# A hybrid decoder step: q and k turned and split in the projection instead of in attention

## The reference, cut to what matters

```
h = rmsnorm(x);  q, k, v, g, z, xbc, dt = split(h @ w_in)        # 1024 x 7696
q, k = rmsnorm per head(q), rmsnorm per head(k)                  # k is also an output
for (window, d) in (128, 1), (512, 4), (2048, 16):               # dilated attention
    query i reads keys i, i-d, i-2d, ..., i-window;  scores * 1/8 + T5 bias(distance)
merge the three outputs by their softmax denominators
a = attention * silu(g)
s = gated rmsnorm(SSD scan(silu(conv(xbc)), dt), z)
y = x + [a, s] @ w_out
```

## Time and profile before

| | us |
|---|---|
| runs (3) | 3159.28, 3165.08, 3168.09; median 3165.08 |
| the profiled execution, its own time | 3156.04 |
| its span, first to last instruction | 3154.4 |
| TensorE matmul busy | 2724.5 (86%) |
| DVE busy | 1305.9 (41%) |
| ACT busy | 941.5 (30%) |
| POOL busy | 788.3 (25%) |
| mean granted TensorE clock | 0.933 of full |

### The profile page before, as it was taken

How to read it: one execution, slowest core, us unless ns; L and a number is a source line. 1 busy time by engine, 2 the same in 40 slices (tenths; PEclk the granted TensorE clock), 3 DMA queues, 4 the chain that set the end, 5 groups by cost and what they waited for, 6 DMA issues and landing times. The chain is left out here.

```text
span 3154.4 us, 48044 instructions
## 1 busy us (share of the span) xinstructions
PE 2724.5 (86%) x16822; PEld 2410.5 (76%) x16822; DVE 1305.9 (41%) x3359; ACT 941.5 (30%) x1999; POOL 788.3 (25%) x533
## 2 busy tenths in 40 slices
PE   7999999999999999978988989889709999505699
PEld 7899999999988888668888878888607888402585
DVE  3254444000000354355656656656326666374321
ACT  3211111221111112125555555545415454200100
POOL 1065565121221231000222122221314434242000
PEclk9999999999999999989999989989959999757899
DMA  4221212321211111182746556464245655383532
GB/s 154 85 75 57 72 58 91 114 70 58 69 58 63 67 53 54 42 148 42 135 73 119 97 86 127 75 107 78 56 146 180 208 199 191 109 310 146 203 146 80
DMA packets 450512, 339.24 MB, mean 108 GB/s; under 512 B 351924, under 2 KB 400412, under 8 KB 442381
## 3 DMA queue, kind: packets, MB, share of 16 engines
q1 hardware_dynamic: 432268, 275.90, 32.6%
q0 software_dynamic: 15424, 56.69, 5.6%
q10 hardware_dynamic: 2672, 4.74, 0.4%
HBM read 242.87 MB, written 99.79 MB: 109 GB/s over the span
## 5 line engine op out<-in xcount | busy, mean ns | idle before, releaser
L118 PE MATMUL bank<-w_hi,hT_hi 128*128 128x256 f32 x1792 | 506.0, 282 | 13.6 <-ACT stage L524 4.7
L120 PE MATMUL bank<-w_hi,hT_lo 128*128 128x256 f32 x1792 | 504.8, 282 | 0.9 <-issue 0.8
L119 PE MATMUL bank<-w_lo,hT_hi 128*128 128x256 f32 x1792 | 503.1, 281 | 0.0
L1059 PE MATMUL obank<-turned_p,v_in 128*128 128x128 f32 (+1 forms) x1632 | 342.1, 344 | 103.2 <-DVE turned_p L1139 97.0
L1059 PEld LDWEIGHTS obank<-turned_p,v_in 128*128 128x128 f32 x1632 | 265.2, 204 | 126.6 <-DVE turned_p L1139 65.2
L118 PEld LDWEIGHTS bank<-w_hi,hT_hi 128*128 128x128 f32 x1792 | 338.8, 189 | 17.3 <-issue 5.6
L120 PEld LDWEIGHTS bank<-w_hi,hT_lo 128*128 128x128 f32 x1792 | 339.4, 189 | 0.0
L119 PEld LDWEIGHTS bank<-w_lo,hT_hi 128*128 128x128 f32 x1792 | 338.7, 189 | 0.0
L1029 PE MATMUL front<-k_hi,q_st 128*128 128x256 f32 x768 | 303.9, 406 | 4.5 <-DVE k_lo L1099 2.8
L1117 DVE CUSTOM_DVE_ANT_0 score<-front,bias_sb 128x256 f32<-128x256 f32 (+1 forms) x768 | 244.5, 362 | 137.6 <-issue 135.6
L602 DVE TENSOR_SCALAR xc<-xc_in,cw,cb 128x2048 f32<-128x2048 f32 x12 | 16.2, 1347 | 642.8 <-ACT xc_in L553 642.8
(11 more groups left out here) (273 smaller groups left out, 5123.7 us busy)
## 6 DMA issues: line engine op xcount, KB each, us to landing
w_raw<-w_in POOLq DMA_DIRECT2D x26, 1024.0 KB
q_in<-q SPq DMA_DIRECT2D x32, 512.0 KB
k_in<-k_out SPq DMA_DIRECT2D x32, 512.0 KB
v_in<-v_out SPq DMA_DIRECT2D x32, 512.0 KB, 7.4
cum_all<-cum SPq DMA_DIRECT2D x16, 1024.0 KB, 7.6
xcT<-xc SPq DMA_DIRECT2D x12, 1024.0 KB, 3.9
xc_chunk<-xcT SPq DMA_DIRECT2D x8, 1536.0 KB, 12.0
kt_d<-cache_k SPq DMA_DIRECT2D x24, 512.0 KB, 8.4
```

The costliest lines, as they stand in the source:

```text
L118: pe.matmul(out, lhs_hi(k), rhs_hi(k), start=k == 0, stop=False)
L119: pe.matmul(out, lhs_hi(k), rhs_lo(k), start=False, stop=False)
L120: last = pe.matmul(out, lhs_lo(k), rhs_hi(k), start=False, stop=k == KT - 1)
L1059: last = pe.matmul(obank[m["bank"]][:, m["col"]:m["col"] + m["n"]], v_in[:, p, m["v"][1], vcols], turned_p[:, g % 4, m["at"]:m["at"] + m[" ...
```

## The change

**Projection.** The normed tiles of q and k go to eight staging buffers (in the space of `xc`). After every four tiles TensorE turns them (eight transposes), ACT takes the high part, DVE the low part, and SP stores both to a scratch `qk` of four parts (q hi, q lo, k hi, k lo), channel-major. DVE sums tile n before it scales tile n-1. The loops of this part are unrolled on all engines. The bias tables move behind the z and v slabs.

```diff
+                def turn(u):
+                    pe.wait_ge(staged, RING * (u + 1))
+                    for c in range(2):
+                        if u >= 1:
+                            pe.wait_ge(qk_split, 2 * (u - 1) + c + 1)
+                        for t in range(RING):
+                            last = pe.transpose(tables[c][:, t * P:(t + 1) * P], qk_stage[:, RING * (u % 2) + t, c * P:(c + 1) * P], ident4[:, :])
+                        last.then_inc(qk_turned, 1)
...
+                        if t % RING == RING - 2 and 1 <= n // RING <= QK_GROUPS:
+                            turn(n // RING - 1)
...
+                def take_high(u):
+                    for c in range(2):
+                        act.wait_ge(qk_turned, 2 * u + c + 1)
+                        if u >= 1:
+                            act.wait_ge(qk_stored[c], 16 * u)
+                        act.copy(qk_parts[:, 0, c, :].bitcast(F32R), tables[c][:, :]).then_inc(qk_high, 1)
...
+                for n in range(NORM):
+                    mean(n)
+                    if n >= 1:
+                        scale(n - 1)
+                    if n % RING == RING - 1 and n >= RING:
+                        take_low(n // RING - 1)
...
+                def store_qk(u):
+                    kind, slab, quad = u // (QK_GROUPS // 2), u // 4 % 4, u % 4
+                    for c in range(2):
+                        sp.wait_ge(qk_split, 2 * u + c + 1)
...
+                        sp.dma_start(dst, qk_parts[:, :, c, :]).then_inc(qk_stored[c], 16)
...
-                            act.activation(xc[:, g * 512:(g + 1) * 512], banks[g][:, :], ACTF.Silu).then_inc(bank_free, 1)
+                            act.activation(residues(xc[:, g * 512:(g + 1) * 512]), by_residue(banks[g][:, :]), ACTF.Silu).then_inc(bank_free, 1)
```

```diff
+        q_st = sb("q_st", [P, 2, SEQ], F32R)
+        k_hi = sb("k_hi", [P, 2, SEQ], F32R)
+        k_lo = sb("k_lo", [P, 2, SEQ], F32R)
...
+    for g in range(NG + 1):
+        due = min(UNITS, -(-UNITS * (g + 1) // NG))
+        n = placed
+        while n < due and freed[n] <= g + 1:
+            n += 1
+        units_at[g] = tuple(range(placed, n if g < NG else UNITS))
+        placed = n
...
+    early = NT - TILES
+    exps_at = {g: range(4 * (g - 10), 4 * (g - 9)) for g in range(10, 18)}
+    own_exps_at = {g: range(early + 2 * g, early + 2 * g + 2) for g in range(8)}
...
+            def load_qk(h):
+                if h >= 2:
+                    act.wait_ge(front_ready, UNITS * (h - 1))
+                for half in range(2):
+                    rows = slice(half * HD, (half + 1) * HD)
+                    for dst, x in ((q_st, half), (k_hi, 2), (k_lo, 3)):
+                        act.dma_start(dst[rows, h % 2, :].bitcast(F32), scr["qk"][x, h * HD:(h + 1) * HD, :]).then_inc(qk_loaded[h % 2], 16)
...
+                    if g == 1 and h + 3 < H:
+                        load_qk(h + 3)
```

```diff
-                        dst = acc[:, b, :].rearrange("p (i r) -> p r i", r=16)[:, 4 * r:4 * r + 4, :]
+                        dst = acc[:, b, :].rearrange("p (q r i) -> p r q i", r=16, i=32)[:, 4 * r:4 * r + 4, :, :]
...
-                        sl = acc[:, b, :].rearrange("p (i r) -> p i r", r=4)[:, :, r]
-                        dve.tensor_tensor(sl, sl, obank[r][:, :], ALU.add).then_inc(o_out[1], 1)
+                        sl = acc[:, b, :].rearrange("p (k a r i) -> p k a r i", a=4, r=4, i=32)[:, :, :, r, :]
+                        dve.tensor_tensor(sl, sl, obank[r][:, :].rearrange("p (k i a) -> p k a i", a=4, i=32), ALU.add).then_inc(o_out[1], 1)
...
-                        dve.tensor_tensor(acc[:, b, cols], acc[:, b, cols], obank[r][:, :], ALU.add).then_inc(o_out[0], 1)
+                        sl = acc[:, b, 512 * r:512 * (r + 1)].rearrange("p (r n i) -> p r n i", r=16, n=4)
+                        dve.tensor_tensor(sl, sl, obank[r][:, :].rearrange("p (n i r) -> p r n i", r=16, n=4), ALU.add).then_inc(o_out[0], 1)
...
-                pool.dma_start(m_raw[:, t % 2, :, :], scr["mT"].rearrange("(m p) t -> p m t", p=P)[:, :, t * P:(t + 1) * P]).then_inc(m_in[t % 2], 16)
+                pool.dma_start(m_raw[:, t % 2, :, :], scr["mT"][t, :, :].rearrange("p (m l) -> p m l", l=P)).then_inc(m_in[t % 2], 16)
```

More of the change, by code:

```diff
@@ L408, in root @@
                     pool.wait_ge(q_sum, n + 1)
[L409 to L423, removed]
+                    pool.tensor_tensor(rsq[:, n % 2, :], msq[:, n % 2, :], mhalf[:, :], ALU.pow).then_inc(q_root, 1)
+                for s in range(QK_SLABS):
+                    b = s % 2
+                    for k in range(KT):
+                        root(s * PER + k)
+                        if k == 0:
+                            pool.wait_ge(w_loaded[1 - b], 16 * ((s + 1) // 2 + 2))
+                        split(s + 1, 1 - b, k=k)
+                    load(s + 3, 1 - b)
+                    for t in range(KT, PER):
+                        root(s * PER + t)
                 first = NORM // PER
@@ L955, in _ @@
             ntop_back(0, 0)
[L956 to L957 removed]
             sp.wait_ge(ntop_loaded, 32)
[L959 to L965 removed]
+            for m in range(H):
+                phase(m, m % 2, m // 2)
             m = H - 1
@@ L1066, in mix @@
                         turn_lot(g)
-                    if more and g < 8:
-                        turn(h + 2, (g,))
                     if g >= 1:
@@ L1075, in _ @@
             for h in range(2):
-                turn(h)
                 scores(h)
-            with pe.Fori(0, H // 2 - 1) as i:
-                mix(2 * i, 0, i)
-                mix(2 * i + 1, 1, i)
-            mix(H - 2, 0, H // 2 - 1, more=False)
-            mix(H - 1, 1, H // 2 - 1, more=False)
+            for h in range(H):
+                mix(h, h % 2, h // 2, more=h + 2 < H)
         @block.vector
@@ L1131, in mix @@
                 for g in range(NG + 1):
-                    if g == 4 and meets:
+                    if g == 5 and meets:
                         meet(h + 1, 1 - b)
```

324 lines of the change are left out of this document (146 added, 178 removed).

## The result

| | before | after |
|---|---|---|
| runs, median (us) | 3162.18 (4 runs) | 3291.22 (4 runs, 3284.69 to 3297.98) |
| profiled execution, own time / span | 3156.04 / 3154.4 | 3291.37 / 3289.6 |
| mean granted TensorE clock | 0.933 | 0.910 |
| PE / DVE / ACT / POOL busy | 2724.5 / 1305.9 / 941.5 / 788.3 | 2707.1 / 1211.7 / 883.1 / 786.2 |

The change is slower: ratio 1.0411, 95% interval 1.0377 to 1.0444. The forecast was 3057 us, its range 2995 to 3130. All three computing engines of attention have less to do than before, as the prediction says, and yet the kernel is 129 us longer by the medians: the time went into waits.

What follows compares the result with a forecast made beforehand. The prediction took TensorE's work plus holes in it as the bound. Attention -113, projection +19, start -7 and tail -7 gave -108 us: 3048 by the profiled execution's own time, 3057 us by the median, range 2995 to 3130.

Steps and rivals of the forecast that it cites:

- Part 3: Attention's q and k loads, six of 512 KB from ACT's queue: 2.2 us of issuing, 1 us a head for collision.
- rival A: In attention, the loads slow the stores of the maxima by some 8 us: 3148 us; chance 0.22 for anything past 3090.
- if an issue took 2 us, it would not: ACT's load issues in a head, priced at 0.366 us, just fit; at 2 us each a head loses up to 5 us.
- Part 1: Attention without turning: 8 groups of transposes go, 3.5 us of TensorE a head, leaving 46.5 of 50.0.
- Part 2: Score units spread over lots 0 to 19 cover the maxima's round trip; a head takes 48.5 us, 8.1 less.
- Part 4: Accumulating by residue in attention: DVE's adds cost +1.8 us a head, none of it on the path.
- The estimate of 1030 ns: By the skill's rule for streams hopping one by one, both kinds of DVE adds in attention land near 1030 ns.
- Part 5: Projection: transposes of q and k add 33 us, holes that go give back 9 and 5; +19 us.
- rival D: Projection: ACT waits for the single-buffered `qk` store when it lands late; at 16 us, 3185 us in all; chance 0.06.
- Part 6, start: Start of attention: 16 groups of turning go, the first load is half as long again; -7 us.
- Tail: End of attention: 16 of ACT's 48 exponentials for the last head move behind; -7 us.
- rows of x and y spread: Scan: spreading the rows of x and y costs 0, within 3 us each way, beside TensorE's work.

Runs made afterwards that it cites:

- e2_sp_same: Changed kernel with the q and k loads issued from SP's queue right behind the stores of the maxima, instead of from ACT's; ratio 1.0423 to the kernel before.
- e12_step12: Changed kernel with q and k loads at step 12, accumulators and scan rows in token order, and the identity's wait moved behind the first products; 3068.3 us.
- e7_units: Changed kernel with loads at step 9 and score units back at two a step from step 8 to 19; ratio 1.0151 to the kernel before, 0.9908 with units spread.
- e5_tokens: Changed kernel with loads at step 9 and accumulators, gate and scan rows by token again, not by residue; ratio 0.9836 to the kernel before, 0.9908 without this undoing.

## Why the prediction was wrong

The step that failed is Part 3, the loads of q and k: the trace "does not price the collision; between 0 and 8 us, I take 1", and rival A with some 8 us. Measured, moving the loads from step 1 to step 9 is worth 158 us by the ratios; between the two profiled executions it is 791.3 - 653.0 = 138 in the passes and 17 on the way into the heads. Per pass that is 10.7 us at step 9 and 12.3 at step 12 (60.9 - 48.6). Two things were missed.

First, only half the round of the maxima was counted. The text lets the loads fly "across the 13 us of those stores". The stores were hardly slowed (14.6 us to 1664.85, against 13.5 in the earlier trace rows); what met the loads in full was the load back, which had been 1.9 us and became 16.4. The rule of the Trainium skill that the prediction cites (DMA: Bandwidth & Descriptors, Queues, rings and completion order), queues taken in turn by the packet, fits a part of this: from 1672 to 1678 us of the head above 189 pieces of 64 bytes and 154 rows of 8 KB begin, about one for one. It does not say why none of the pieces began before 1671.0. The rival had a chance of 0.22 and a ceiling drawn from the overlap with the stores; that the round is a store and a load in sequence, and that the loads of q and k begin to move only when the stores are nearly through, was not counted.

Second, ACT's issue was priced from a quiet moment (0.366 us). Behind SP's stores of the maxima and its load of the bias the six took 12.4 us by the median, with loads of 8 KB up to 8.5. e2_sp_same shows that this is not paid on top. The prediction named the case ("if an issue took 2 us, it would not" fit) and gave it no term of the sum.

The other steps:
- Part 1 (turning out of attention, 46.5 us of TensorE a head): right, 46.9 busy at the lower clock, 45.3 at step 12.
- Part 2 (a head of 48.5 us; the units cover the round): right once the loads are elsewhere, 48.6 us in e12_step12 with 3.3 of them idle (2.5 forecast), 46.2 without their bytes. That the units are what covers the chain is shown by e7_units; the worth of it is 3.1 us a pass and 6 on the way in with the loads at step 9. The clock did not come to the 0.97 asked for (0.95 over the passes at step 12).
- Part 4 (residue adds, 0 on the path, dearer on DVE): nearly right on the path, where they gave 7 us (e5_tokens), wrong in sign on DVE: 683 ns for the four adds for which 1131 was taken, 680 for the four that had cost 1131. The estimate of 1030 ns, from what the Trainium skill (Vector Engine (DVE) Microarchitecture Reference, Measured stream behaviour on trn2) states for streams in SBUF, is not borne out where only the PSUM side has the step.
- Part 5 (+19 for q, k, z, v): right, +14.6. The slabs of q and k took 17.3 us more (24 by the terms; the listed sign was 20 to 30), those of z and v 2.7 less (5). A turn of eight transposes costs 0.80 us between two products, 26 in all, where 33 were forecast; the products kept their 281 ns. The `qk` store landed after 5.0 us by the median, 9.3 at most. The sign of rival D did show, ACT waited for it 33 times, 63.4 us in all, but TensorE did not miss ACT, so the rival did not come.
- Part 6, start (-7, with the first pass -15): +25.5, of which 17 went with the loads' place. The rest, 24 us against the forecast, is open. Tail (-7): right, -4.3.
- Part 6, "rows of x and y spread: 0, within 3 us": wrong, +32.4. Here the change of the DMA's axes was seen and only its bytes and row length were weighed, which stayed the same. The scan has no room: from 2400 to 2686 us of the kernel before TensorE was busy all the time, at full clock.
- The first wait for the identity, +11.3: missed. It was in the diff as one line ahead of a loop; the DMA that it waits for is the fifth that SP issues in this part, at 149.06 us.

By terms, all against the forecast of -108 and from the profiled executions: the loads' place, step 1 for step 9, +155 (138 and 17), the scan +32, the identity +11, the way into the heads a further +24 (25.5 + 15, less the 17 that the place explains), and +21 that the 13 passes still lose at step 9 with the residue part against step 12 without it (653.0 and 632.0 us). That leads to +135, as measured. With the loads at step 12, the scan in order and the identity moved, the seven spans of the table read 142.7, 706.5, 501.4, 148.6, 632.0, 64.4 and 871.6 us, -87 in all: the 13 passes give -106 where -105 were forecast, and what is short is the way in (+8 for -15), the last two heads (-3 for -7) and the channel-major part (+2), against which q, k, z and v took 5 less than forecast.

The signs listed ahead of time: DVE's reduce came 31.1 us after the first store of the maxima, where "more than 18" was to show rival A; and ACT's issues were far from 0.37 us. PE's wait for DVE's copy was below 3 us a head, as asked, since the wait had moved to `front` and to ACT.

## What to carry to other kernels

In this kernel the round trip of small DMAs through DRAM is a chain that ends waits on every engine. Keep a large load out from between its first store and its last load back; it made no difference here on which of the two queues it was issued. Price it by the landing of the small DMA that comes after, not by that of the large one, and look for the first step behind the last landing; here two steps made 78 us.

When a change regroups the rows of a DMA, read the size of the outermost axis before the bytes. And look at where an engine that computes issues its DMAs: behind SP's small stores and its next load, six issues took ACT 12.4 us instead of 3.9.

## What the runs showed of the hardware

- Six loads from ACT's queue took 0.62 us each to issue in quiet (512 KB). When SP had just issued three stores of 2048 maxima each, in pieces of 4 to 64 bytes, and a load of 320 KB, the six took 12.4 us by the median (512 KB) or 1.7 to 8.5 us (8 KB). The largest single issue in the kernel after was 8.6 us. Issued by SP itself (e2_sp_same) the six took 11.1 us.
- SP's issues were long beside ACT's loads too: at the start of attention in the kernel after the load of the gate at 1413.10 took 13.00 us to issue, with 3 MB issued by ACT from 1411.7 on (2.35 us in the kernel before), and the two loads of v at 1372.12 took 26.04 us, with 6 MB issued by ACT from 1369.4 on (3.44 us).
- A 24 KB load in runs of 64 bytes landed in 1.9 us alone and in 16.4 us beside 3 MB in rows of 8 KB.
- 256 KB in 128 rows of 2 KB landed in 3.1 to 3.4 us with 32 or 128 rows on the outermost axis, in 7.8 with 4.
- DVE adding a bank of 512 read at a step in PSUM into runs in SBUF took 680 ns; with the bank read in order and a step of 4 elements in SBUF, read and written, 1131.
